# The opening of a decoder-layer kernel: five weight blocks in four strips instead of three blocks in five, with kept partial sums and interleaved column sums

## What is computed

```
cond = silu(c)
mod = cond @ ada_w + ada_b                     # 2048 x 18432, nine vectors of 2048
sh1, sc1, gt1, sh2, sc2, gt2, sh3, sc3, gt3 = split(mod, 9)
x = sandwich(x, swiglu(ffn1_w_in, ffn1_w_out), g0, g1, sh1, sc1, gt1, 0.5)
x = sandwich(x, token_mixer(...),              g2, g3, sh2, sc2, gt2, 1.0)
x = sandwich(x, swiglu(ffn2_w_in, ffn2_w_out), g4, g5, sh3, sc3, gt3, 0.5)
# sandwich: h = rms_norm(x, g_pre) * (1 + scale) + shift;  x + w * gate * rms_norm(fn(h), g_post)
# swiglu:   gate, up = split(h @ w_in, 2);  (silu(gate) * up) @ w_out      with D_FF = 5504
```

## Time and profile before

| | us |
|---|---|
| median of 3 runs | 1907.82 |
| profiled execution, its own time | 1910.38 |
| its span in the profile | 1908.6 |
| TensorE busy | 1864.7 (98%) |
| VectorE busy | 1470.7 (77%) |
| ScalarE busy | 857.9 (45%) |
| mean granted TensorE clock | 0.992 |

### The profile page before, as it was taken

The page is one execution under the profiler, slowest core; times in us unless marked ns, Lnnn a source line. Parts: engine busy times, 40 slices in busy tenths (PEclk is TensorE's granted clock), DMA queues, the critical chain, the costliest instruction groups (busy, mean ns, idle before and its releaser), DMA issues.

```text
span 1908.6 us, 21980 instructions
## 1 busy us (share of the span) xinstructions
PE 1864.7 (98%) x8775; PEld 1567.9 (82%) x8775; DVE 1470.7 (77%) x1569; ACT 857.9 (45%) x1095; POOL 82.0 (4%) x151
## 2 busy tenths in 40 slices
PE   6999999999999999999999999999999999999997
PEld 6887888888888889878888887888888888888895
DVE  5988889798888889965776587677867785676576
ACT  4244443443443434574666545544344434443443
POOL 0001000000000000010000010000000000000000
PEclk9999999999999999999999999999999999999999
DMA  9999999999999989655444444766677655556552
GB/s 368 374 370 343 355 340 342 353 333 348 347 341 346 371 325 347 247 165 176 146 133 133 160 155 151 246 242 235 234 250 251 240 180 198 197 191 213 177 202 77
DMA packets 208677, 486.84 MB, mean 255 GB/s; under 512 B 8560, under 2 KB 29760, under 8 KB 193472
## 3 DMA queue, kind: packets, MB, share of 16 engines
q1 hardware_dynamic: 191648, 365.72, 55.3%
q0 software_dynamic: 16224, 117.47, 16.7%
q10 hardware_dynamic: 704, 2.25, 0.3%
HBM read 483.31 MB, written 2.10 MB: 254 GB/s over the span
## 4 chain that ended last, share of the span: by engine, by line
PE 91%; DVE 4%; DMA 2%; issue 1%; ACT 1%; ACTq 0%; SPq 0%; DVEq 0%; POOL 0%
PE ps_u L1551 10%; PE ps_u L1553 10%; PE ps_u L1552 10%; PE ps_g L1551 9%; PE ps_g L1553 9%; PE ps_g L1552 9%; PE ps_t L1551 4%; PE ps_t L1553 4%; PE ps_t L1552 4%; PE ps_y L1553 4%; PE ps_y L1552 4%; PE ps_y L1551 4%; DVE arena L1267 1%; PE ps_g L1649 1%; PE ps_t L1820 1%
## 5 line engine op out<-in xcount | busy, mean ns | idle before, releaser
L595 ACT ACTIVATE w_hi<-w_raw 128x1024 fp32r<-128x1024 f32 (+2 forms) x604 | 629.0, 1043 | 881.2 <-PE ps_u L1553 308.5
L977 DVE TENSOR_TENSOR w_lo<-w_raw,w_hi 128x1024 fp32r<-128x1024 f32 (+2 forms) x604 | 719.7, 1200 | 356.5 <-ACT w_hi L595 354.4
L1551 PE MATMUL ps_u<-w_hi,xT_hi 128*128 128x512 f32 (+2 forms) x880 | 345.1, 392 | 4.0 <-DVE arena L1033 1.8
L1553 PE MATMUL ps_u<-w_hi,xT_lo 128*128 128x512 f32 (+2 forms) x880 | 339.4, 386 | 0.0
L1552 PE MATMUL ps_u<-w_lo,xT_hi 128*128 128x512 f32 (+2 forms) x880 | 338.9, 385 | 0.0
L1551 PE MATMUL ps_g<-w_hi,xT_hi 128*128 128x512 f32 (+1 forms) x816 | 319.1, 391 | 0.5 <-DVE w_lo L977 0.4
L1553 PE MATMUL ps_g<-w_hi,xT_lo 128*128 128x512 f32 (+1 forms) x816 | 314.6, 386 | 0.0
L1552 PE MATMUL ps_g<-w_lo,xT_hi 128*128 128x512 f32 (+1 forms) x816 | 314.1, 385 | 0.0
L1011 DVE SCALAR_TENSOR_TENSOR arena<-ada_raw,cond,arena 128x2048 f32<-128x2048 f32 x108 | 253.4, 2347 | 4.6 <-DMA ada_raw<-in_ada_w 4.5
L1551 PEld LDWEIGHTS ps_u<-w_hi,xT_hi 128*128 128x128 f32 x880 | 165.5, 188 | 35.8 <-DVE arena L1033 2.2
L1553 PEld LDWEIGHTS ps_u<-w_hi,xT_lo 128*128 128x128 f32 x880 | 165.6, 188 | 32.2
(11 more groups left out here) (316 smaller groups left out, 1905.5 us busy)
## 6 DMA issues: line engine op xcount, KB each, us to landing
w_raw<-in_ffn_w_in SPq DMA_DIRECT2D x157, 1024.0 KB, 6.6
ada_raw<-in_ada_w POOLq DMA_DIRECT2D x112, 1024.0 KB, 6.2
w_raw<-in_ffn_w_out SPq DMA_DIRECT2D x80, 1024.0 KB, 6.5
w_raw<-in_mix_w_in SPq DMA_DIRECT2D x32, 1024.0 KB, 5.1
ada_raw<-in_ada_w SPq DMA_DIRECT2D x32, 512.0 KB, 8.9
arena<-in_ada_w SPq DMA_DIRECT2D x32, 512.0 KB, 9.6
w_raw<-in_mix_w_out SPq DMA_DIRECT2D x16, 1024.0 KB, 5.0
w_raw<-in_ffn_w_in SPq DMA_DIRECT2D x16, 768.0 KB, 5.4
```

The costliest lines, as they stand in the source:

```text
L595: nc.scalar.activation(w_hi[:, u % 4, 0:n, 0:width], w_raw[:, s, 2 * hf:2 * hf + n, 0:width], ACT.Copy).then_inc(hi_done, 3 if g in EARLY_ ...
L977: nc.vector.tensor_tensor(w_lo[:, u % 4, 0:n, 0:width], w_raw[:, s, 2 * hf:2 * hf + n, 0:width], w_hi[:, u % 4, 0:n, 0:width].bitcast(F32) ...
L1551: nc.tensor.matmul(o, a_hi[:, k, rows], w_hi[:, b, c, 0:width], start=start, stop=False)
L1553: ins = nc.tensor.matmul(o, a_lo[:, k, rows], w_hi[:, b, c, 0:width], start=False, stop=stop)
```

## The change

`STRIP_CHUNKS` becomes four strips of 4 chunks, and `OPENING` 5: gate 0, up 0, gate 1, up 1 and gate 2 are all worked in the opening, 40 units instead of 24. TensorE has accumulators for three of them (`KEPT`); the other two share `ps_y` in turn (blocks 3 and 4 by `block_of`). In each strip but the last, ScalarE copies their sums out (`save_partial`, 128 x 1024), and in the next strip TensorE puts them back by a float32 product with the identity (`take_partial`, two products of 512 columns). The order of blocks in a strip is 0, 3, 1, 4, 2, so the last two units belong to `ps_t` and `ps_y` is free for column sums. The 16 column-sum products of the next strip are no longer a run of their own but stand between the 12 products of the last-but-one unit of the strip (`unit_with_sums`), which waits for all tiles of the next strip, for the second saved sum and for `warm(20)` in the first strip and `warm(3)` in the two after. SyncE puts each strip's weight load ahead of the tile load that it followed. VectorE's order within a strip and the accumulators of the tiles (`even`, now `acc[:, 1]`; `odd`) are written anew. In the steady stretch one tile of ada_w falls on 2.2 units instead of 2.4, the first row turn moves from block 3 to 4 (`ROWS_AT`), and two groups fewer follow; GpSimd clears the gate accumulators later, between its loads.

```diff
-ROWS_AT = (3, 5, 7, 9)
+ROWS_AT = (4, 5, 7, 9)
...
-STRIP_CHUNKS = ((0, 4), (4, 4), (8, 4), (12, 2), (14, 2))
+STRIP_CHUNKS = ((0, 4), (4, 4), (8, 4), (12, 4))
 STRIPS = len(STRIP_CHUNKS)
-FULL = sum(n == 4 for _, n in STRIP_CHUNKS)
-OPENING = 3
+OPENING = 5
+KEPT = 3
+BLOCK_COLS = (0, DFF, NB, DFF + NB, 2 * NB)
+STRIP_UNITS = 2 * OPENING
...
+MODS_LATER = ((3, 1), (4, 3), (6, 2), (7, 3), (2, 1), (5, 0), (8, 3))
...
-UNIT_FFN1 = [12 * a // 5 for a in range(6 * KD)]
+UNIT_FFN1 = [11 * a // 5 for a in range(6 * KD)]
...
+def block_of(s, i):
+    return (0, 3, 1, 4, 2)[i] if s < STRIPS - 1 else i
...
+        even = acc[:, 1, :].rearrange("p (s m n) -> p s m n", s=2, m=2)
+        odd = junk.rearrange("p (s m n) -> p s m n", s=2, m=2)
+        partial = acc[:, 2, :].rearrange("p (e t n) -> p e t n", e=2, t=TILES)
...
+            def first_weights(s, i):
+                q, col, chunk = OPENING * s + i, BLOCK_COLS[block_of(s, i)], STRIP_CHUNKS[s][0]
                 need(sp, lo_done, 2 * (q - 4) + 2)
-                sp.dma_start(w_raw[:, q % 4, 2 * hf:2 * hf + chunks, :], win_v[0][:, chunk:chunk + chunks, col:col + NB]
-                             ).then_inc(w_landed[q % 4] if s < FULL else half_landed[v - 2 * OPENING * FULL], 16)
+                sp.dma_start(w_raw[:, q % 4, :, :], win_v[0][:, chunk:chunk + 4, col:col + NB]).then_inc(w_landed[q % 4], 16)
...
             for s in range(STRIPS):
                 more = s + 1 < STRIPS
+                first_weights(s, 0)
                 if more:
                     first_tile(s + 1, 0)
...
+                first_weights(s, 1)
...
+                first_weights(s, 4)
+                for i in range(4, STRIP_TILES[s + 1] if more else 0):
                     first_tile(s + 1, i)
...
+            def save_partial(s, e):
+                act.wait_ge(pe_used, STRIP_UNITS * s + 4 * e + 4)
+                nc.scalar.activation(partial[:, e, :, :], ps_y[:, :, :], ACT.Copy).then_inc(partial_saved, 1)
...
+                start = STRIP_UNITS * s
                 first_hi(start)
-                if s >= STRIPS - 2:
-                    first_xt_hi(STRIP_CHUNKS[s][0] // 2)
-                    first_hi(start + 1)
-                    first_hi(start + 2)
-                    continue
-                for i in range(1, units):
+                first_hi(start + 1)
+                first_xt_hi(2 * s)
+                first_hi(start + 2)
+                first_xt_hi(2 * s + 1)
+                for i in range(3, 6):
                     first_hi(start + i)
-                    if 2 * i - 2 < STRIP_CHUNKS[s][1]:
-                        first_xt_hi(STRIP_CHUNKS[s][0] // 2 + i - 1)
-            act.wait_ge(pe_used, 7 * OPENING + 1)
+                if s < STRIPS - 1:
+                    first_hi(start + 6)
+                    first_hi(start + 7)
+                    save_partial(s, 0)
+                    first_hi(start + 8)
+                    first_hi(start + 9)
+                    save_partial(s, 1)
+            act.wait_ge(pe_used, 8 * OPENING - 8)
...
+                start, more = STRIP_UNITS * s, s + 1 < STRIPS
                 first_lo(start)
                 first_lo(start + 1)
                 first_columns(s)
-                first_xt_lo(first_xt)
-                if tiles:
+                if more:
+                    first_ada(s + 1, 0)
+                first_xt_lo(2 * s)
+                first_lo(start + 2)
+                first_xt_lo(2 * s + 1)
+                if more:
                     first_ada(s + 1, 1)
-                    done = 2
-                for i in range(2, units):
-                    first_lo(start + i)
-                    if 2 * i - 2 < STRIP_CHUNKS[s][1]:
-                        first_xt_lo(first_xt + i - 1)
-                    late = i - units // 2 + 1
-                    upto = 2 + (tiles - 2) * late // (units - units // 2) if tiles and late > 0 else done
-                    for t in range(done, upto):
-                        first_ada(s + 1, t)
-                    done = upto
+                first_lo(start + 3)
+                first_lo(start + 4)
+                if not more:
+                    for i in range(5, 8):
+                        first_lo(start + i)
+                    h_mul(0, 0, NB, start + 4)()
+                    first_lo(start + 8)
+                    first_lo(start + 9)
+                    continue
+                first_ada(s + 1, 2)
+                first_lo(start + 5)
+                first_lo(start + 6)
+                first_ada(s + 1, 3)
+                first_lo(start + 7)
+                first_lo(start + 8)
+                first_ada(s + 1, 4)
+                first_lo(start + 9)
+                for i in range(5, STRIP_TILES[s + 1]):
+                    first_ada(s + 1, i)
...
+            def column_sum(s, i):
+                (m, c), part = divmod(i // 2, 4), (even, odd)[i % 2]
+                k = STRIP_CHUNKS[s][0] + c
+                return nc.tensor.matmul(ps_y[:, 0, m * KD + k:m * KD + k + 1], part[:, s % 2, m, c * P:(c + 1) * P], ones[:, 0:1],
+                                        start=i % 2 == 0, stop=i % 2 == 1)
+            def sums_free(s):
                 pe.wait_ge(ada_done, first_count(s, STRIP_TILES[s] - 1))
                 need(pe, modcol_done, s)
-                odd = junk.rearrange("p (s m n) -> p s m n", s=2, m=2)
-                for m in range(2):
-                    for c in range(chunks):
-                        k = chunk + c
-                        col = ps_y[:, 0, m * KD + k:m * KD + k + 1]
-                        nc.tensor.matmul(col, acc[:, MODS_PRE[m][1], k * P:(k + 1) * P], ones[:, 0:1], start=True, stop=False)
-                        ins = nc.tensor.matmul(col, odd[:, s % 2, m, c * P:(c + 1) * P], ones[:, 0:1], start=False, stop=True)
-                ins.then_inc(cols_done, 1)
+            def unit_with_sums(s, pair, v, ps):
+                done = 0
+                for t in range(TILES):
+                    for c in range(2):
+                        k, rows = 2 * pair + c, slice(t * P, (t + 1) * P)
+                        for n, (x, w) in enumerate(((xT_hi, w_hi), (xT_hi, w_lo), (xT_lo, w_hi))):
+                            ins = nc.tensor.matmul(ps[:, t, :], x[:, k, rows], w[:, v % 4, c, :], start=k == 0 and n == 0, stop=False)
+                            for _ in range(2 if n == 2 else 1):
+                                col = column_sum(s, done)
+                                done += 1
+                ins.then_inc(pe_used, 1)
...
+                col.then_inc(cols_done, 1)
...
+            def take_partial(e, ps):
+                for t in range(TILES):
+                    nc.tensor.matmul(ps[:, t, :], ident[:, :], partial[:, e, t, :], start=True, stop=False)
             warm(12, ps_g)
-            first_sums(0)
+            sums_free(0)
+            for i in range(16):
+                ins = column_sum(0, i)
+            ins.then_inc(cols_done, 1)
...
+                last = s == STRIPS - 1
+                if s:
+                    pe.wait_ge(modcol_done, s + 1)
+                    pe.wait_ge(partial_saved, 2 * s)
+                    take_partial(0, ps_y)
+                for i in range(STRIP_UNITS):
+                    v, (q, hf) = STRIP_UNITS * s + i, divmod(i, 2)
+                    b, pair = block_of(s, q), 2 * s + hf
+                    ps = (ps_g, ps_u, ps_t, ps_y, ps_g if last else ps_y)[b]
+                    if b == KEPT + 1 and hf == 0:
+                        if last:
+                            pe.wait_ge(silu_done, 2)
+                            transpose_h(0, 4, 0)
+                        else:
+                            pe.wait_ge(partial_saved, 2 * s + 1)
+                        if s:
+                            take_partial(1, ps)
                     pe.wait_ge(lo_done, v + 1)
+                    if i == STRIP_UNITS - 2 and not last:
+                        pe.wait_ge(partial_saved, 2 * s + 2)
+                        warm((20, 3, 3)[s], ps_y)
+                        sums_free(s + 1)
+                        unit_with_sums(s + 1, pair, v, ps)
+                        continue
                     if b == 0:
                         high_first_unit(pair, v, ps)
                         continue
                     pe.wait_ge(xt_lo_done, pair + 1)
-                    unit(xT_hi, xT_lo, 2 * pair, v % 4, 2, NB, lambda t: ps[:, t, :], pair == 0, pair == KD // 2 - 1).then_inc(pe_used, 1)
+                    unit(xT_hi, xT_lo, 2 * pair, v % 4, 2, NB, lambda t: ps[:, t, :], v // STRIP_UNITS == 0 and hf == 0,
+                         pair == KD // 2 - 1 if b < KEPT else hf == 1).then_inc(pe_used, 1)
```

More of the change, by code:

```diff
@@ L225, in build @@
         w_landed = [sem(f"w_landed{s}") for s in range(4)]
-        half_landed = [sem(f"half_landed{i}") for i in range(2 * OPENING)]
         ada_landed = [sem(f"ada_landed{s}") for s in range(4)]
@@ L1025, in y_add, with h_mul @@
                 return f
```

(27 more changed lines are left out.)

129 lines of the change are left out of this document (49 added, 80 removed).

## The result

The changed kernel takes 1918.84 us (median of 4 runs, 1917.78 to 1920.06) against 1907.65 us of the kernel before (4 runs beside it): ratio 1.0056, 95% interval 1.0044 to 1.0067, so 11 us slower. The forecast was 1903.3 with a range of 1897 to 1916; the result lies outside it. The profiled execution took 1918.47 us (span 1916.7), 8.1 us more than that of before.

The account below looks back on a forecast made before the run. TensorE was taken to bound the steady stretch, so the change pays through the opening: 194.7 - 190.2 = 4.5 us less, profiled 1905.9, median 1903.3 us, range 1897 to 1916.

Parts of the forecast that it names:

- Clock kept: Forecast case: TensorE stays at full clock in the opening's units with sums; chance 0.50, own range 1897 to 1907 us.
- The first rival: TensorE's clock falls in units with sums: 5 us a strip; one fall 1908.3 (0.16), two 1913.3 (two or more 0.28).
- Spreading the sums is less idle than a run: Argument against a clock fall in the unit with sums: interleaved column sums leave TensorE less idle than a run.
- The sum for a kept clock: Opening's steps added at full clock: the 40th unit ends at 190.2 us, against 194.7 for no gain; 4.5 us less.
- A put-back: TensorE's return of a saved sum by two float32 products of 512 columns: 1.7 us, bounds 1.0 to 2.2.
- The step from the profile to the median: Whole-kernel time: profiled execution 1905.9 us, the median taken as 2.6 us under it, 1903.3.
- Steady stretch: After the opening: VectorE's 3% more is hidden by TensorE's lead; DMA rises from 347 to 361 GB/s, taken as free.
- the DMA rival: Steady stretch becomes DMA's if 347 GB/s is its limit: 4% of 575 us lost, 1926 us; chance 0.06.
- the case of a limit of 358 GB/s: Steady stretch: if the skill's HBM figure held, 361 GB/s would be 0.9% too much: 5 us, time 1908.
- sums nearly free: Rival for units with sums: at 0.11 us a sum they end 1.2 us earlier, 1899 to 1900; chance within 0.50.
- The opening doesn't get denser: Rival for the strips: three limits of 36 to 37.4 us meet, hand-overs add 1 us each, 1906.5; chance within 0.50.
- The rule cited in the prediction: Skill's rule that copying a result out of PSUM doesn't break TensorE's warmth; by it the saved sums are harmless.

Follow-up runs that it names:

- w9: The changed kernel with nine instead of three warm (dummy) products ahead of the units with sums of the second and third strip: 1905.68 us.
- run9: w9 with the sixteen column sums as a run ahead of the plain unit instead of between its products, in all three strips: 1914.51 us.
- w6: The changed kernel with six instead of three warm products ahead of the units with sums of the second and third strip: 1905.42 us.
- even3: The changed kernel, warm products 20, 3, 3, with the eight even sums first and the unit waiting only for the even partial sum: 1903.16 us.
- early0: even3 with 10, 0 and 0 warm products, and the unit's first two products without sums: 1904.88 us.
- nosum: The changed kernel with 14 of the 16 column sums of strips 1 to 3 left out, so scale and shift are wrong: 1897.52 us.

## Why the prediction was wrong, point by point

**The failed step is the clock in the units with sums.** "Clock kept" had half of the chance and gave the forecast. The wait for the saved sum, the three warm products and VectorE's lateness were priced at their own length only. The forecast itself listed 1.3 us idle, 0.7 us warm and up to 0.9 us idle; measured are 1.21, 0.7 and 1.14. The first rival had the mechanism, the place and the sign, with a chance of 0.28 for two falls and a time of 1913.3; it was too cheap. A fall was priced at 4 us in the unit and 2 in the next, less 1 that VectorE's slack would take: 5. Measured, the unit grows by 4.9 (11.3 against w9's 6.4) and the next by 1.5 to 1.6, and nothing absorbs any of it: 6.4 a fall. Three strips are 5.4 + 6.8 + 1.8 = 14.1 us (rounded) longer than forecast, 12.9 longer than in w9.

**"Spreading the sums is less idle than a run"** is true (run9: three falls, w9: none) and was no protection: I compared the interleaving with the run it replaces, and not with what the changed unit has in front of it. In the first strip 20 warm products stand there, in the others three.

**The sum for a kept clock was right.** w9 is that case: shift and scale at 80.17, 118.08 and 155.95 (forecast 81.4, 118.8, 156.2), unit with sums 6.36 us (6.1), 40th unit's end at 190.19, the start of the first output product:

```profile
190.19 0.39 PE L1543 MATMUL ps_y<-w_hi,hT_hi 128*128 128x512 f32 x1
```

The forecast was 190.2, partly by errors that cancel: w9's first shift and scale starts 1.5 us earlier (40.82 against 42.34), its first strip is 0.3 longer, the next two 0.5 each (37.9 against 37.4) and the last 0.2. The terms that were mis-sized are small. A put-back takes 83.09 - 81.78 = 1.31 us (1.7 forecast, bounds 1.0 to 2.2), in the changed kernel's rows:

```profile
81.78 1.88 PE L1800 MATMUL ps_y<-arena,ident 128*128 128x512 f32 x4
83.09 0.79 PE L1788 MATMUL ps_g<-w_hi,xT_hi 128*128 128x512 f32 x1
```

The 0.22 us of a sum were read as 67.44 - 67.22, while the earlier trace rows have 67.47; the unit bears them out all the same, (6.36 - 2.72) / 16 = 0.23.

**The step from the profile to the median was off too.** By profiles w9 gains 1910.38 - 1905.39 = 5.0 us, by medians 1.9. The execution of before that was profiled is at the upper end of its runs (in the later sets 1905.88 to 1911.88), w9's at the lower end of its own. I carried the 2.6 us offset of before over to the changed kernel as if it were fixed. Part of it may be clock, since the low stretch at the start of the first strip was 10.2 us in that execution and 6.8 in w9's. It can't be much of it, for the runs of before all have a mean clock of 0.991 to 0.993, and the profiled one 0.992. Where the rest comes from is open. So even with the clock kept the time is 1905.4 to 1905.7 (w6, w9), 2 us above the forecast and not the "faster" (below 1904.0) that it stood for.

**What held.** Steady stretch: TensorE busy for 200.0 of 200.0 us and in every window to 700 us, at 354 to 371 GB/s (361 forecast). That ends the DMA rival, and the case of a limit of 358 GB/s with it. VectorE waits 7.8 us for its tiles between 215 and 800 us, TensorE has no wait for DMA. Last strip: 34.2 us in w9 (34.0). The "sums nearly free" rival is refuted by the unit's 6.3 us at full clock. "The opening doesn't get denser" gave 1906.5, near w9's 1905.68, but by another way: the strips have their forecast length.

**The wait behind the copy did no harm where dummy products followed it.** The rows of w6, w9 and even3 have the 1.21 us wait behind ScalarE's copy out of PSUM in every strip and clock 1.00 behind it. The rule cited in the prediction (the Trainium skill, "TensorE: Matmul & The Clock Gate", Loop structure matters more than you think) agrees with these, though its case is a copy by VectorE that the next products don't wait for. In the changed kernel the same copy is followed by a second wait and narrow products, and the clock falls; that the copy did no harm there does not make the hand-over harmless. In early0 the wait of 1.2 us stands alone ahead of the unit in the second and third strip, with no dummy products behind it, and the clock falls for 3.4 us at the end of both units. To take the saved sums for harmless by that rule was a step that the rule's own case doesn't carry.

## What to carry to other kernels

When an edit puts waits and narrow products next to each other on TensorE, add up the idle time ahead of the narrow stretch place by place, and price the clock's fall as the likely case where two such gaps meet (here 1.21 and 1.14 us). Fill the second gap first with the unit's own work (wait only for the half of the input that the first instructions read), then with dummy products up to the moment when the input is there and not beyond. Read a low stretch in a profile as something that may be shorter or longer in the next execution (3.4, 6.8 and 10.2 us at one place here), and look at each run's mean clock before you call a scatter noise or a fall.

## What the runs showed of the hardware that was not expected

- TensorE's clock fell without any idle time directly ahead: within a run of 16 sums (4.2 to 4.5 us) to 0.50 for 6.8 us, three times of three (run9).
- Little separates the two cases: 1.21 + 1.14 us of idle time ahead of the unit with sums went with 13.6 us at 0.50 in both strips, 1.21 + 0.47 us with none (w6).
- A low stretch under wide products alone was 3.4 us (nosum), one under the unit with sums 13.6 us (changed kernel, twice).
- A sum between wide products costs 0.22 to 0.23 us (w9 and the changed kernel), the same as in a run: 16 of them make the unit 6.3 us instead of 2.7.
